# Closing a decoder step: residual by identity matmuls, final norm with tokens on partitions, stores from SyncE's queue

## The reference, cut to what matters

```
x = x + mem_attention(rms_norm(x, g_mem), ...)
x = x + hier_moe(rms_norm(x, g_ffn), ...)     # sum over the two chosen experts
...
y = rms_norm(x, final_norm_g)                 # x * rsqrt(mean(x*x) + eps) * g
return (y_prompt, y_sample, states and key/value rows)
```

## Time and profile before

| | |
|---|---|
| median of 3 timed runs | 1505.09 us |
| the three runs | 1508.72, 1505.09, 1489.38 us |
| the profiled execution | 1494.2 us, span 1492.3 us |
| its granted TensorE clock, mean | 0.926 |
| PE, DVE, ACT, POOL busy, share of the span | 87%, 40%, 27%, 10% |
| DMA | 339.64 MB, mean 228 GB/s |
| chain that ended last | PE 65%, DMA 17%, DVE 10%, ACT 3% |

### The profile page before, as it was taken

The page is one execution under the profiler, slowest core; times in us unless marked ns, Lnnn a source line. Parts: engine busy times, 40 slices in busy tenths (PEclk is TensorE's granted clock), DMA queues, the critical chain, the costliest instruction groups (busy, mean ns, idle before and its releaser), DMA issues.

```text
span 1492.3 us, 20803 instructions
## 1 busy us (share of the span) xinstructions
PE 1296.9 (87%) x8388; PEld 795.5 (53%) x8388; DVE 595.5 (40%) x1184; ACT 407.5 (27%) x704; POOL 145.0 (10%) x186
## 2 busy tenths in 40 slices
PE   5799999998877799999989869859887869999994
PEld 4676688766656333333357557636665633333333
DVE  2554476754334322112344655415433432211113
ACT  3443331553332111111243214344333211111112
POOL 5100031100001011101010420000000101110100
PEclk9799997999987899999999979959998879999998
DMA  8465353558652099999835646104865208999971
GB/s 241 140 203 141 114 158 118 185 163 289 226 234 116 1 369 427 425 427 427 347 113 156 211 156 226 57 1 129 322 226 227 123 0 356 427 427 426 426 304 37
DMA packets 112230, 339.64 MB, mean 228 GB/s; under 512 B 7406, under 2 KB 75322, under 8 KB 83456
## 3 DMA queue, kind: packets, MB, share of 16 engines
q1 hardware_dynamic: 106560, 320.89, 56.8%
q0 software_dynamic: 5136, 16.26, 3.2%
q10 hardware_dynamic: 432, 1.11, 0.2%
HBM read 327.69 MB, written 10.54 MB: 227 GB/s over the span
## 4 chain that ended last, share of the span: by engine, by line
PE 65%; DMA 17%; DVE 10%; ACT 3%; issue 3%; SPq 1%; POOL 1%; POOLq 0%; DVEq 0%; ACTq 0%
DMA arena<-in_w_exp_up 14%; PE ps L1927 11%; PE ps L523 8%; PE ps L525 8%; PE ps L524 8%; PE ps L1912 2%; PE ps L1976 2%; PE ps L1433 2%; PE ps L1489 2%; PE ps L1408 2%; PE ps L1956 2%; PE ps L1394 2%; PE ps L757 2%; PE ps L1473 1%; DVE wl L517 1%
## 5 line engine op out<-in xcount | busy, mean ns | idle before, releaser
L1927 PE MATMUL ps<-arena,mkv 128*64 128x512 f32 x1024 | 231.4, 605 | 23.4 <-DMA arena<-in_w_exp_up 17.2
L523 PE MATMUL ps<-bx,wh 128*128 128x320 f16 (+1 forms) x640 | 194.2, 303 | 41.0 <-DVE bx L748 15.5
L524 PE MATMUL ps<-bx,wh 128*128 128x320 f16 (+1 forms) x640 | 194.0, 303 | 0.0
L525 PE MATMUL ps<-bx,wl 128*128 128x320 f16 (+1 forms) x640 | 194.0, 303 | 0.0
L517 DVE SCALAR_TENSOR_TENSOR wl<-stg,wh 128x1024 f16<-128x1024 f32 x128 | 157.8, 1272 | 85.7 <-ACT wh L510 85.0
L510 ACT ACTIVATE wh<-stg 128x1024 f16<-128x1024 f32 x128 | 128.4, 1049 | 215.5 <-PE ps L525 191.1
L1927 PEld LDWEIGHTS ps<-arena,mkv 128*64 128x64 f32 x1024 | 81.8, 139 | 168.9 <-issue 161.6
L2065 DVE TENSOR_TENSOR arena<-ps,arena 128x512 f16<-128x512 f32 x64 | 44.1, 689 | 143.2 <-ACT arena L2031 92.4
L523 PEld LDWEIGHTS ps<-bx,wh 128*128 128x128 f16 x640 | 64.9, 101 | 67.1 <-issue 34.7
L523 PE MATMUL ps<-arena,wh 128*128 128x320 f16 x288 | 87.0, 302 | 3.7 <-DVE arena L1356 3.0
L524 PE MATMUL ps<-arena,wh 128*128 128x320 f16 x288 | 86.9, 302 | 0.0
(11 more groups left out here) (396 smaller groups left out, 1881.5 us busy)
## 6 DMA issues: line engine op xcount, KB each, us to landing
arena<-in_w_exp_gate SPq DMA_DIRECT2D x64, 1024.0 KB, 14.8
arena<-in_w_exp_up SPq DMA_DIRECT2D x64, 1024.0 KB, 16.8
arena<-in_w_exp_down SPq DMA_DIRECT2D x32, 1024.0 KB, 17.3
stg<-in_w_exp_down SPq DMA_DIRECT2D x32, 1024.0 KB, 16.8
arena<-in_cache_mem_k SPq DMA_DIRECT2D x16, 1024.0 KB, 7.2
arena<-in_cache_mem_v SPq DMA_DIRECT2D x16, 1024.0 KB, 5.0
stg<-in_w_in_a SPq DMA_DIRECT2D x28, 512.0 KB, 4.7
stg<-in_w_qkv_c SPq DMA_DIRECT2D x20, 512.0 KB, 4.7
```

What stands on the lines that cost most here:

```text
L523: nc.tensor.matmul(out, wh[:, s, at:at + 128], hi, start=start, stop=False)
L524: nc.tensor.matmul(out, wh[:, s, at:at + 128], lo, start=False, stop=False)
L525: return nc.tensor.matmul(out, wl[:, s, at:at + 128], hi, start=False, stop=stop)
L1927: last = nc.tensor.matmul(ps[64 * j:64 * j + 64, UB, :], xe[:, q % 2, j, k, :], gu[:, g % 2, j, :, k, :], start=(k == 0), stop=(k == KD - ...
```

## The change

Three parts.

In layer 1 alone, PE opens the five PSUM banks with the residual before any expert output is added: `seed` multiplies slices of `xT` by the identity, 24 f32 matmuls of 128 columns, after `transpose_h(0)` and before `up(1)`. `combine(0)` then adds to the banks where it started them before. The banks hold the new residual stream at the end, so layer 1 has no `unpack_*`.

The final norm works on the banks, tokens on partitions. ACT squares each bank with a running sum over its 512 columns into a column of the new tile `fin`; DVE adds the two halves of the first two blocks; PE adds the two halves of the last block by a matmul with `fold_pair`; ACT takes the root; DVE scales each bank by the token's factor and by `gfin`, the gain vector repeated on all 128 partitions, which POOL loads with a DMA ahead of `rc`. This takes the place of `norm_pe`, `norm_dve`, the 24 transposes and their copies.

The outputs are stored in six DMAs from SP, each after its piece is scaled, in place of two from POOL after all of them.

```diff
+    take = area(0, mkv[:, 1])
+    gfin = take(1024)
+    junk = take(5, 512)
+    take = area(0)
+    yout = take(5, 512)
...
+    HALVES = ((0, 0, 0), (1, 0, 1), (2, 1, 0), (3, 1, 1), (4, 2, 0), (4, 2, 1))
+
+    def final_sp(sp):
+        for b, i, half in HALVES:
+            c = slice(512 * half, 512 * half + 512)
+            sp.wait_ge(S["xn_ready"], XN[6] + 1 + b + (half if i == 2 else 0))
+            if i < 2:
+                sp.dma_start(o["y_prompt"][0, 128 * i:128 * i + 128, c], yout[:, b, :]).then_inc(S["out_y"], 16)
+            else:
+                sp.dma_start(o["y_sample"].rearrange("b i d -> (b i) d")[:, c], yout[64 * half:64 * half + 64, b, :]
+                             ).then_inc(S["out_y"], 16)
+        sp.wait_ge(S["out_y"], 16 * len(HALVES))
...
+        def seed():
+            for i, (t0, n) in enumerate(TILES):
+                for half in range(2):
+                    out = ps[64 * half:64 * half + 64, 4, :] if i == 2 else ps[:, 2 * i + half, :]
+                    for j in range(4):
+                        nc.tensor.matmul(out[:, 128 * j:128 * j + 128], xT[:, 4 * half + j, t0:t0 + n], ident,
+                                         start=(j == 0), stop=False, skip_group_check=True)
+
         def combine(q):
             pe.wait_ge(M["y_lo"], 2 * q + 2)
-            first, final = q == 0, q == last_step
+            first, final = q == 0 and l == 0, q == last_step
...
         select(0)
         transpose_h(0)
+        if l == 1:
+            seed()
         for q in range(1, last_step + 1):
...
+    def final_pe(pe):
+        pe.wait_ge(S["hsq_ready"], HA + 2)
+        for half in range(2):
+            last = nc.tensor.matmul(ps[64 * half:64 * half + 64, 7, 0:1], const("fold_pair"), fin[:, 4:5], start=True,
+                                    stop=True, skip_group_check=True)
+        last.then_inc(S["sum_ready"], 1)
+
+    def final_act(act, link):
+        act.wait_ge(S["z_ps"], 2)
+        for b in (4, 0, 1, 2, 3):
+            ins = nc.scalar.activation(junk[:, b], ps[:, b, :], ACT.Square, accum_out=fin[:, b:b + 1])
+            if b in (4, 3):
+                ins.then_inc(S["hsq_ready"], 1)
+        act.wait_ge(S["sum_ready"], 7)
+        nc.scalar.activation(fin[:, 10:11], ps[:, 7, 0:1], ACT.Ln, bias=epsc[:, 0:1], scale=1.0 / D)
+        act.wait_ge(S["zs_dve"], 3)
+        link(nc.scalar.activation(fin[:, 8:10], fin[:, 6:8], ACT.Ln, bias=epsc[:, 0:1], scale=1.0 / D))
+        nc.scalar.activation(fin[:, 12:15], fin[:, 8:11], ACT.Exp, scale=-0.5).then_inc(S["std_ready"], 1)
+
+    def final_dve(dve):
+        dve.wait_ge(S["hsq_ready"], HA + 3)
+        nc.vector.tensor_tensor(fin[:, 6:8], fin[:, 0:4:2], fin[:, 1:4:2], ALU.add).then_inc(S["zs_dve"], 1)
+        dve.wait_ge(S["std_ready"], 13)
+        dve.wait_ge(S["gate_in"], 48)
+        for b, i, half in HALVES:
+            rows = slice(64 * half, 64 * half + 64) if i == 2 else slice(0, 128)
+            nc.vector.scalar_tensor_tensor(yout[rows, b, :], ps[rows, b, :], fin[rows, 12 + i:13 + i],
+                                           gfin[rows, 512 * half:512 * half + 512], ALU.mult, ALU.mult
+                                           ).then_inc(S["xn_ready"], 1)
...
         pool.wait_ge(S["in_lo"], sum(IN["memo1"]))
+        pool.dma_start(gfin, a["final_norm_g"].partition_broadcast(128)).then_inc(S["gate_in"], 16)
         pool.dma_start(rc, a["slots"]).then_inc(S["rc_in"], 16)
...
-        pool.wait_ge(S["tr_ev"], G_Y + 6)
-        pool.dma_start(o["y_prompt"][0].rearrange("(t p) d -> p t d", p=128), x_nat[:, 0:2, :]).then_inc(S["out_y"], 16)
-        pool.dma_start(o["y_sample"].rearrange("b i d -> (b i) d"), x_nat[0:64, 2, :]).then_inc(S["out_y"], 16)
-        pool.wait_ge(S["out_y"], 32)
```

More of the change, by code:

```diff
@@ L155, in build @@
     rtok = sb("rtok", [128, 2, 3])
+    fin = sb("fin", [128, 16])
     xn = bx[:, 0:KD * T].rearrange("p (k t) -> p k t", k=KD)
@@ L502, in _ @@
                     sp.wait_ge(dw_used, NPAIR)
+                else:
+                    final_sp(sp)
     def split_hi(act, u, s, src=None):
@@ L791, in norm_tok_act @@
         act.wait_ge(S["std_ready"], 2 * n + 2)
[L793 to L797, removed]
     def sum_pe(pe, n):
@@ L817, in sum_pool @@
                                     ).then_inc(S["acc_ready"], 1)
[L819 to L827, removed]
     SMALL = 16 * 4
@@ L2190, in pe_memory @@
         moe(pe, l, moe_pe)
-        unpack_pe(pe, l)
+        if l == 0:
+            unpack_pe(pe, l)
     def pe_rest(pe):
@@ L2204, in pe_rest @@
         pe_memory(pe, 1)
[L2205 to L2211, removed]
+        final_pe(pe)
     def act_memory(act, link, l):
@@ L2222, in act_memory @@
         moe(act, l, moe_act)
-        unpack_act(act, l)
+        if l == 0:
+            unpack_act(act, l)
     def act_rest(act, link):
@@ L2236, in act_rest @@
         act_memory(act, link, 1)
-        act.wait_ge(S["moe_done"], 4)
-        nc.scalar.activation(sq[:], xT[:], ACT.Square).then_inc(S["sq_ready"], 1)
-        norm_root_act(act, 6)
+        final_act(act, link)
     def dve_memory(dve, link, l):
@@ L2249, in dve_memory @@
         moe(dve, l, moe_dve)
-        unpack_dve(dve, l)
+        if l == 0:
+            unpack_dve(dve, l)
     def dve_rest(dve, link):
@@ L2261, in dve_rest @@
         dve_memory(dve, link, 1)
[L2262 to L2268, removed]
+        final_dve(dve)
     def pool_rest(pool, link):
```

## The result

The changed kernel takes 1484.47 us, the median of 20 runs (1474.1 to 1492.67), beside 1497.09 for the kernel before in the same session (20 runs, 1488.99 to 1508.72). The ratio is 0.9918, 95% interval 0.9892 to 0.9943, so -12.3 us (-16.2 to -8.5). That is within 2%; 1492 was forecast from a starting median of 1505.1, and -12.8 as the difference. Its profiled execution took 1490.5, span 1489.1; 1494.2 and 1492.3 before.

A forecast was written before the change was run, and what follows sets the result against it. Bound by the weight stream in layer 1's experts, then a 31.6 us relay after the last combine. Seed +5.6 and tail -18.4 sum to -12.8, giving 1492 from the 1505.1 median; range 1473 to 1501.

The forecast's parts named there:

- tail, all: After the last combine: a new relay of 13.2 us replaces the old 31.6, saving 18.4.
- seed at pair 1: Layer 1 before `up(1)`: 48 instructions at 0.128 take 6.1 us, less a filled 0.51 pause, net +5.6 to the end.
- rival 1's second form: Seed at layer 1's start: the filled gap keeps the clock up; 1487 to 1491 us, chance 0.13 shared with the other form.
- the lower bound of 3.9: Seed before `up(1)`: smallest delay, 5.6 - 1.7 = 3.9 us, if the filled gap keeps the clock at 2.4 GHz.
- The signs: Layer 1: seed 6.1 to 7.9 us, `up(1)` near 7.1, pair 3's load near 1251.0, last `up` 5.6 later.
- A hole in the stream decides who pays: Layer 1's weight stream: without holes from 1254 on, it hands any delay before pair 3's load to the end, +5.6 us.
- Rival 1's first form: Layer 1: PE's 8.7 us of weight waits swallow the seed; 1487 to 1491 us, chance 0.13 shared with the other form.
- Rival 2: Seed in layer 1 costs more, 8.7 us if bound by weight loads, or partly at 1.2 GHz; 1495 us, chance 0.13.
- Rival 3: Longer tail: table-switch pauses +2.6, accumulator reads +1.0, last store +1.8; all three 1498 us; chance 0.09, pause alone 0.04.
- Rival 4: Seed at 1.2 GHz throughout with weight loads not overlapped costs 19.2 us, net +0.8, 1506 us; chance 0.02.
- Rival 5: Tail's six stores land one behind another, 17.4 us; tail 24.5, net -1.5, 1504 us; chance 0.03.
- Costs at nothing: Gain vector's 512 KB broadcast on POOL ahead of `rc`: covered by idle POOL and DMA, 0 us; uncovered up to 1.8.

The follow-up runs named there:

- before_shifted: Kernel before with an unused tile of 64 bytes a partition in the place of `fin`; 1505.25 us, ratio 1.0056.
- seed_only: Kernel before with only the seed added, old norm and stores; layer 1's last unpack copies instead of adding; 1498.40 us, ratio 0.9990.
- fin_behind: Changed kernel with the tile `fin` declared behind the large ones, so `arena` returns to its old address; 1481.61 us, ratio 0.9898.
- no_seed: Changed kernel without the 24 identity matmuls, so the residual is missing from the outputs; 1486.51 us, ratio 0.9897.
- late_seed: Changed kernel with the seed cut into six groups of four matmuls ahead of `up(9)` to `up(14)`; 1486.16 us, ratio 0.9902.
- gap_seed: table_in_branch with two of its six seed groups moved between `select(0)` and `transpose_h(0)`; 1474.97 us, ratio 0.9829.
- late_behind_table: Changed kernel with late seed groups, `fin` behind `arena`, and an unused logarithm before ScalarE's wait for the last sums; 1478.24 us, ratio 0.9844.
- table_in_branch: late_behind_table with the unused logarithm moved inside layer 1's branch, behind ScalarE's last copy; 1480.21 us, ratio 0.9881.

## Why the prediction was right, and where it was not

The forecast difference, -12.8, lies near the measured -12.3, but that is partly luck: two of its terms were wrong in opposite directions. With layer 0's stream, which the table of pieces leaves out, the account is:

| step | predicted | measured |
|---|---|---|
| squares | 3.0 | 3.00 |
| first table load | 1.28 | 1.28 |
| logarithms, switch, exponential | 1.93 | 1.97 |
| six scalings | 3.9 | 4.17 |
| last store exposed | 2.9 | 2.3 |
| handovers between engines | 0.2 | 0.1 |
| tail, all | -18.4 | -18.8 |
| seed at pair 1 | +5.6 | +2.65 |
| weight stream, layer 1 | 0 | +2.66 |
| weight stream, layer 0 | 0 | +2.75 |
| sum | -12.8 | -10.7 |

-10.7 is inside the measured interval (-16.2 to -8.5). The old tail could account for 1.4 of the 1.6 us to its middle: with the 33.01 of before_shifted in place of 31.58 the sum is -12.1. Which of its values is usual in the timed runs is not shown. The time itself, 1484.5, lies 7.6 below the 1492 forecast, since the median of three runs from which it was counted (1505.1) lay 8 above that of twenty.

*The tail: right in mechanism and in size.* The last scaling ended 10.5 us after the last combine, 10.3 predicted. Each scaling took a little more than interpolated from 256 and 640 columns; the store from SyncE's queue took less than the 2.3 fixed plus 0.6 for its bytes. Both bounds of the store (1.5 and 4.7) held.

*The seed: the step that failed* is "I let that stretch of 1.2 GHz fall on the seed instead of on `up(1)`, at the same cost of 1.7 us, so it cancels." It does not fall on either. In all four profiles with the early seed (the changed kernel twice, seed_only, fin_behind) the granted clock is 1.00 from 3 to 7.5 us after the load for pair 2; in all three without it (before, no_seed, late_seed) it lies between 0.50 and 0.73 in that stretch. The size per instruction was off too: 48 in a row take 5.08 us until `up(1)`, 0.106 each and not 0.128. The row it came from was read rightly, for 16 instructions: 16 of the seed's take the same 2.05 us in gap_seed, and 8 take 1.16 (0.145 each) in late_seed. Each lasts 272 to 323 ns by the profile and overlaps the next; the price of one falls with the number in a row. Seed and old pause and clock together, 5.1 - 0.5 - 1.8 = 2.8, explain the 2.65; the other 0.17 is that the seed starts 0.34 after the transposes do, before they end. This is rival 1's second form ("the filled gap keeps the clock up"); the lower bound of 3.9 did not hold, since it kept the price of 0.128. Why the low clock follows a pause here is not shown; that it is absent once the pause of 0.51 (early seed) or of 1.76 us (gap_seed) is filled with matmuls is.

*The signs.* The last `up` came 5.3 us later, and 5.6 was named; the number is right by luck, for the seed gives 2.65 of it and the slower stream 2.66. SyncE's load for pair 3, named for near 1251.0 (17.4 after the one for pair 2), came 14.44 after it, which is where the seed's error shows.

*A hole in the stream decides who pays: right.* The seed's delay reached the last combine whole (no_seed against the changed kernel), although PE waited 11.1 us for weights after it. Rival 1's first form, that these waits swallow the seed, fell. late_seed showed the other side: behind the hole the same work is free.

*Rivals.* Rival 2, more than 5.6, fell with 5.1 us for 48 instructions. Rival 3's pause at the table switches fell: 0.01 to 0.02 us stand on each side of both loads, and nothing longer; its accumulator reads overlap. Rival 4 fell with the clock of 1.00. Rival 5 fell: the stores overlap, the last lands 2.3 us after its piece.

*Costs at nothing.* The broadcast of the gain vector held: one issue of 0.59 us on POOL at 1150.34, landed in 8.4 us beside the loads for pairs 0 and 1 (399 GB/s in 1150:1159). They were in by 1180 all the same; in 1180:1200 the engines move 3 GB/s, the cover that the prediction counted on. "Nothing" was also what I had for one thing I did not see as an edit: the new declaration `fin`. It moves the place of every expert weight in `arena` by 64 bytes and costs 2.66 + 2.75 = 5.4 us, twice what the seed does. The stages ahead of layer 0's experts were not compared. No row of before could have shown it; the diff could have raised the question.

## What to carry to other kernels

A new tile in front of large DMA targets moves them all. An offset of 64 bytes cost `arena` 1.24% of its stream, one of 256 nothing, and no other offset was tried; so declare small tiles behind the buffers that bulk loads fill, and compare GB/s in a stretch that the change does not touch. Price added work by where it stands against the next hole in the stream, not by the total of the engine's waits: ahead of the hole it is paid whole, behind it, it was free here or nearly so, and in a pause of the engine itself it even gave time back through the clock. When two terms of a sum are uncertain, check them one by one after the result; a right total does not vouch for either.

## What was not expected of the hardware

- 64 bytes of offset in SBUF take the weight loads from 426 to 421 GB/s at a busy share of 1.01 in both cases; 256 bytes take nothing.
- 2 us of f32 matmuls in a pause of 1.76 us, or 5.1 us of them in one of 0.51, and the clock stays at 2.4 GHz (granted 1.00) where it otherwise lies at 0.50 to 0.73 for some 4 us: worth 1.7 us of `up(1)` (8.78 to 7.03).
- An f32 matmul of 128 columns is two instructions, at that clock 0.106 us each with 48 in a row and 0.145 with 8, with weight loads of 0.19 hidden.
- The ones-matmuls of the old norm, the same 16 instructions, took 6.28 to 7.37 us from profile to profile, at a mean granted clock of 0.73 down to 0.62.
- A running sum on ScalarE costs no time beside the square: five of 512 columns in 3.00 us, with an accumulator read of 0.19 inside each next one.
- ScalarE idled 2.13 us between its last instruction in the layer's branch and the first behind it (late_behind_table); with a table load inside the branch it idled 1.78 there, until PE was done (table_in_branch).
